# Eighteen unread products on TensorE ahead of the first weight unit, and the input's sum of squares one block of the contraction later

## The reference

```python
def _rmsnorm(x, g):
    y = xf * lax.rsqrt(jnp.mean(xf * xf, axis=-1, keepdims=True) + EPS)
    return (y * g).astype(x.dtype)
...
u = _rmsnorm(h, g_mix_pre[i])
z = u @ w_in[i]
a_b, a_c, a_x, q_lat, kv_lat, k_rope, gate_a, gate_b = jnp.split(z, split_pts, axis=-1)
q = (_rmsnorm(q_lat, g_q_lat[i]) @ w_q_up[i])
```

## Time and profile before

| | |
|---|---|
| median of 3 runs | 1718.85 us |
| lowest, highest | 1718.37, 1720.22 us |
| the profiled execution | 1719.0 us |
| its span, first to last instruction | 1717.1 us |
| TensorE matmul, busy share of the span | 98% |
| VectorE, GpSimd, ScalarE | 57%, 57%, 36% |
| mean granted TensorE clock (share of full speed) | 0.998 |
| HBM traffic over the span | 88 GB/s |

### The profile page before, as it was taken

One profiled execution on the slowest core, in us unless ns is written; L12 is line 12 of the kernel. 1 busy time (PEld: TensorE's weight loads), 2 busy tenths in 40 slices (PEclk: granted clock), 3 DMA queues, 4 the chain that ended last, 5 costly groups with the idle time before them and its releaser, 6 DMA issues.

```text
span 1717.1 us, 22045 instructions
## 1 busy us (share of the span) xinstructions
PE 1688.8 (98%) x7846; PEld 1401.7 (82%) x7846; DVE 977.1 (57%) x1635; ACT 610.1 (36%) x1159; POOL 973.8 (57%) x586
## 2 busy tenths in 40 slices
PE   7999999999999999998999999999999999999998
PEld 6788788788888888887788888888888888888887
DVE  7778443345651554255847544537667967776244
ACT  4455311243312222043723322322534127765022
POOL 5545466656666666664765566545564653333654
PEclk9999999999999999999999999999999999999999
DMA  5212222322233222322222222222232221111222
GB/s 204 82 58 75 88 93 95 98 92 93 98 98 102 95 97 98 111 93 89 100 86 75 74 86 99 74 86 74 87 105 86 87 95 53 50 50 62 86 88 85
DMA packets 51943, 152.25 MB, mean 89 GB/s; under 512 B 11152, under 2 KB 12304, under 8 KB 51728
## 3 DMA queue, kind: packets, MB, share of 16 engines
q1 hardware_dynamic: 50992, 149.50, 26.4%
q10 hardware_dynamic: 864, 1.57, 0.3%
HBM read 148.95 MB, written 2.10 MB: 88 GB/s over the span
## 4 chain that ended last, share of the span: by engine, by line
PE 94%; DVE 3%; issue 1%; ACT 1%; DMA 0%; POOL 0%; SPq 0%; DVEq 0%; POOLq 0%; ACTq 0%
PE bank L779 28%; PE bank L781 28%; PE bank L780 28%; PE bank L1587 1%; PE bank L1192 1%; PE bank L1193 1%; PE bank L1196 1%; PE bank L1430 1%; PE bank L1426 1%; PE bank L1427 1%; PE bank L817 1%; PE bank L803 1%; PE bank L935 0%; DVE fx L2417 0%; PE bank L1089 0%
## 5 line engine op out<-in xcount | busy, mean ns | idle before, releaser
L749 POOL TENSOR_SCALAR w_hi<-raw 128x1024 fp32r<-128x1024 f32 (+1 forms) x279 | 293.2, 1051 | 671.7 <-issue 487.0
L751 POOL TENSOR_TENSOR w_lo<-raw,w_hi 128x1024 fp32r<-128x1024 f32 (+1 forms) x279 | 657.3, 2356 | 23.3
L779 PE MATMUL bank<-op_hi,w_hi 128*128 128x512 f32 x984 | 390.8, 397 | 9.6 <-DVE op_lo L2417 8.7
L781 PE MATMUL bank<-op_hi,w_lo 128*128 128x512 f32 x984 | 384.2, 390 | 0.0
L780 PE MATMUL bank<-op_lo,w_hi 128*128 128x512 f32 x984 | 384.1, 390 | 0.0
L779 PE MATMUL bank<-r,w_hi 128*128 128x512 f32 x856 | 339.2, 396 | 1.7 <-POOL w_lo L751 1.6
L781 PE MATMUL bank<-r,w_lo 128*128 128x512 f32 x856 | 333.9, 390 | 0.0
L780 PE MATMUL bank<-r,w_hi 128*128 128x512 f32 x856 | 333.7, 390 | 0.0
L779 PEld LDWEIGHTS bank<-op_hi,w_hi 128*128 128x128 f32 x984 | 185.5, 189 | 48.0 <-ACT fx L1726 8.7
L781 PEld LDWEIGHTS bank<-op_hi,w_lo 128*128 128x128 f32 x984 | 185.2, 188 | 39.2
L780 PEld LDWEIGHTS bank<-op_lo,w_hi 128*128 128x128 f32 x984 | 185.5, 189 | 37.2 <-issue 1.0
(11 more groups left out here) (278 smaller groups left out, 2315.6 us busy)
## 6 DMA issues: line engine op xcount, KB each, us to landing
raw<-in_weights SPq DMA_DIRECT2D x268, 512.0 KB, 3.3
out<-h SPq DMA_DIRECT2D x8, 256.0 KB, 2.0
h<-in_x SPq DMA_DIRECT2D x3, 512.0 KB, 7.2
raw<-in_weights SPq DMA_DIRECT2D x8, 192.0 KB, 2.4
cst<-in_consts SPq DMA_DIRECT2D x1, 1156.5 KB, 10.0
rope_cos<-in_p ACTq DMA_DIRECT2D x3, 256.0 KB, 3.5
rope_sin<-in_p ACTq DMA_DIRECT2D x3, 256.0 KB, 3.7
h<-in_x SPq DMA_DIRECT2D x2, 256.0 KB, 4.0
```

The source lines that it names most:

```text
L749: pool.tensor_scalar(hi, raw[:, r, at:w], 1.0, 0.0, ALU.mult, ALU.add).then_inc(hi_ready, 1)
L751: pool.tensor_tensor(lo, raw[:, r, at:w], hi.bitcast(F32), ALU.subtract).then_inc(split_ready, 1)
L779: pe.matmul(o, ah, bh, start=start, stop=False, skip_group_check=skip)
L781: return pe.matmul(o, al, bh, start=False, stop=stop, skip_group_check=skip)
```

## The change

Three edits. VectorE clears a 128 x 512 tile `still_tile` at its very start and signals `still`. TensorE waits for that, and multiplies the tile with itself 18 times into PSUM bank 6, which nothing reads before it is overwritten. `blockwise` is counted in contraction blocks k rather than in units, and the sum of squares comes behind k = 4 instead of behind k = 3. The order of the blocks is unchanged.

```diff
+        still_tile = r2[:, 0:T]
...
+        still = sem("still")
...
-            def blockwise(u0, before, units=range(4)):
+            def blockwise(u0, before, parts=M8):
 
                 d = S[before]["dve"]
-                for c in units:
+                for k in parts:
+                    c, kk = k // 2, k % 2
                     pe.wait_ge(split_ready, u0 + c + 1)
-                    for kk in range(2):
-                        k = 2 * c + kk
-                        pe.wait_ge(d.sem, d.at(f"lo{k}"))
-                        for m in range(4):
-                            mm = split_mm(ps[m][:, :], w_hi[:, (u0 + c) % 2, 4 * kk + m], w_lo[:, (u0 + c) % 2, 4 * kk + m],
-                                          op_hi[:, k], op_lo[:, k], k == 0, k == KD - 1)
-                    mm.then_inc(unit_done, 1)
-
+                    pe.wait_ge(d.sem, d.at(f"lo{k}"))
+                    for m in range(4):
+                        mm = split_mm(ps[m][:, :], w_hi[:, (u0 + c) % 2, 4 * kk + m], w_lo[:, (u0 + c) % 2, 4 * kk + m],
+                                      op_hi[:, k], op_lo[:, k], k == 0, k == KD - 1)
+                    if kk:
+                        mm.then_inc(unit_done, 1)
+
+            pe.wait_ge(still, 1)
+            for n in range(18):
+                pe.matmul(ps[6][:, :], still_tile[:, 0:P], still_tile, start=n == 0, stop=n == 17)
             a, d, z = enter(pe, "pe", "start")
-            blockwise(U0["lat"], "start", range(2))
+            blockwise(U0["lat"], "start", range(5))
             pe.wait_ge(cst_in, 16)
             pe.wait_ge(d.sem, d.at("acc7"))
             z.done(full_sum(4), "sum")
-            blockwise(U0["lat"], "start", range(2, 4))
+            blockwise(U0["lat"], "start", range(5, KD))
...
+            dve.memset(still_tile.bitcast(F32), 0.0).then_inc(still, 1)
             clear(st[:, 63:64])
             dve.wait_ge(gain_in, 16)
```

## The result

The changed kernel took **1727.21 us** (median of 6 runs, 1724.08 to 1728.14), the kernel before 1719.49 (6 runs, 1718.37 to 1720.22): ratio 1.0041, 95% interval 1.0031 to 1.0051. It is slower, as forecast, but by 7.7 us where 5.5 were forecast, and the time lies 1.2 us above the range. The profiled execution took 1727.26 us, with a span of 1725.5. Lines behind the diff are a few numbers higher: L779 to L781 are now L781 to L783, L797 is L799, L803 is L805, L817 is L819, L2417 is L2422.

The account below looks back on a forecast made before the run. TensorE carries 94% of the chain of waits, but must wait for VectorE's `acc2`; resuming 3.6 us later plus 1.9 for the clock gave 5.5 on 1719.0, 1724.5, less 0.15 for the median: 1724.4 us, range 1719.8 to 1726.0.

Parts of the forecast that it names:

- The ramp and the warm-up: TensorE's start: unread products raise the clock before 8.74 us, no delay, and blocks 0 to 3 end 2.1 us earlier.
- Unit 2 and the sum: Block 4: unit 2's landing holds its split to 16.3 to 16.5; sum of squares at 23.3, 1.4 us later.
- The splits on the angles: VectorE's angles: unit 5's GpSimd split lengthens them, 2.2 us; with the later sum, TensorE resumes 3.6 us later.
- The clock after the wait: Behind TensorE's wait for `acc2`: the clock falls to its lower level, costing 1.9 us, bounds 0 and 2.1.
- What follows is dense: Claim about TensorE's work behind the wait for `acc2`, made in taking 1.9 us for the clock's fall.
- Later stages ... all shift together: Behind 38.42 us: every wait stands against an engine that follows TensorE, so all moves by the same 5.5 us.
- The sum: Forecast total: 3.6 us later at TensorE's resumption plus 1.9 for the clock, 5.5 us slower.
- (B): Behind the wait for `acc2`: the chain gets longer but the clock holds, 1722.5 us; chance 20%.
- (D): At the start: products of a cleared tile don't raise the clock, 7.3 us slower, 1726.3 us; chance 9%.
- (C): VectorE's angles escape GpSimd's splits, the chain ends 1.4 us earlier, 1717.6 us; chance 10%.

Follow-up runs that it names:

- the 18 products alone: Changed kernel with the sum of squares put back behind block 3, the 18 products kept: 1719.69 us, ratio 0.9999 to the kernel before.
- the split held back: Changed kernel with GpSimd starting unit 5's split only after VectorE's `clip`: 1723.74 us, ratio 1.0016 to the kernel before.
- the wait filled: Changed kernel with 20 more unread products of the cleared tile just ahead of the wait for `acc2`: 1723.25 us, ratio 1.0017 to the kernel before.
- the control: Kernel before with only its angles moved to PSUM, no unread products, sum behind block 3: 1719.03 us, ratio 0.9991 to the kernel before.
- the moved sum alone: Kernel before with the sum of squares behind block 4, no cleared tile or 18 products: 1728.03 us, ratio 1.0045 to the kernel before.
- the mid-block version: Changed kernel with angles in PSUM and the sum after two of block 4's four output blocks: 1718.04 us, ratio 0.9990 to the kernel before.

## Why the prediction was wrong in size and right in kind

- **The ramp and the warm-up**: right. No delay, a warm start; 0.94 us of idle ahead of 8.49 did not cool it.
- **Unit 2 and the sum**: right. Split at 16.57, released by its data (forecast 16.3 to 16.5), sum at 23.35 (23.3).
- **The splits on the angles**: right. Unit 5's split at 32.76 (32.8), `sin` at 37.73 (38.0), 1.9 net for the splits (2.2), wait of 5.08 (5.2), `sum_q` 3.31 later (3.6). Holding the split and moving the data to PSUM both remove it.
- **The clock after the wait**: this is the step that failed. It took 1.9 us from the stretch of 791 us and 2.1 from the ramp as the upper bound. It measured 3.65, and 3.66 in the second profile. That a fall would come was right; its size, a term of the sum, was about half of what it should have been. The two rows that I had were of starts with 512-column matmuls at once, and the prediction says "What follows is dense"; here TensorE restarts with eight products of one column, 1.87 us long, and has eight of 128 columns among the rest, and it is 7.5 us until the clock returns, not 4. Whether those small products are the cause was not tried and stays open. The nearest pair on record points that way: after a wait of 2.21 ahead of the sum and 512-column matmuls (the 18 products alone) the fall cost 1.45, and after 2.30 ahead of `sum_q` (the split held back) 3.2; but these are single executions, and the price differed by 1.2 among three waits of 5.08 to 5.10 ahead of the same products. An upper bound taken from two rows of another mix was no bound.
- **"Later stages ... all shift together"**: failed by 1.2. The fall near 790 was there in both kernels but began earlier against the work (the eight products of L819 took 2.08 instead of 1.36 in the kernel before) and ended later. No run shows that the change did this. Measured over the same work, this stretch was as long as in the kernel before, within 0.1 us, in four of the other profiled executions (the wait filled, two of the versions with the angles in PSUM, and the control), and 0.9 to 1.5 longer in the rest, the 18 products alone among them. It should have been in the range as a cost that can move.
- **The sum**: -0.3 (`sum_q`), +1.75 (clock) and +1.2 (second fall) make 2.65 us, of the 2.8 by which the profiled executions differ from the forecast 5.5.
- **The rivals**: holding the clock (B) was wrong; products that don't raise it (D) were wrong, though its time, 1726.3, was the closest; the escape from the splits (C) was seen only when the data were moved, and the kernel was then level with the kernel before, not faster. What spoke for (B), a wait of 1.27 that kept the clock, was no safe sign: after waits of 1.30 and 1.31 ahead of `sum_q` it fell. The kind, slower by over 0.2%, was right.

## What to carry to other kernels

Before speeding up the busiest engine in one stretch, find where it next waits: here it was 0.37 us ahead of a serial chain on other engines, so the saved time could only turn into waiting, and starting that chain later to fill the gap cost more than the gap. When a step is moved, look at what every other queue does at the new time: GpSimd's work for the next unit slid onto VectorE's angles. If a chain is slow because two engines get in each other's way at SBUF, try its data in PSUM before reordering anything. And give the cost of a fall of the clock a wide range: the next kernel's mix of matmuls may not be that of the row it is taken from.

## What the runs showed of the hardware

- Matmuls of an all-zero tile raised TensorE's clock: 18 of them took 6.09 us, and the next ones ran 0.23 apart.
- The climb of the clock at the start differed between executions: the first 10 intervals were at the lower level's pace in the kernel before, 14 with the moved sum alone and 7 in the control, and the 18 products took 5.75 to 7.06 us in eleven profiled executions.
- The price of one fall of the clock ahead of the same work was 1.6, 1.6, 2.5, 3.2, 3.4 and 3.65 us in the profiled executions of six kernels, after waits of 1.31, 1.30, 5.09, 2.30, 5.10 and 5.08 (each is the gauge less 6.03). The length of the wait alone doesn't set it. None was paid where products left 0.56, 0.41 or 0.27 of the wait.
- Falls came ahead of 512-column matmuls as well, after waits of 2.21 and 1.82 (the 18 products alone, the mid-block version), though not after 0.94 and 0.84 in the changed kernel. The Trainium skill ("TensorE: Matmul & The Clock Gate", on HAM oscillation) places the danger in long gaps; here 1.3 us of waiting, followed by eight one-column products, was enough twice. The measurement decides: a short wait isn't safe.
- Beside a GpSimd tensor_tensor a VectorE tensor_scalar from SBUF to SBUF took 2.50 us, and with its output in PSUM 0.75; a scalar_tensor_tensor on SBUF took 2.77, and with one input and the output in PSUM 0.72.
- The granted clock reads 1.00 over 8 to 13 us in the kernel before, while the starts there are at the lower level's pace.
